# Value products four steps behind the scores in place of two, in the attention stage of a hybrid block on one Trainium2 core

## The reference

```python
def hybrid_layer(x, positions, ...):
    h = rmsnorm(x, g_norm_mix)
    proj = h @ w_in                       # split into 14 parts
    ...
    y_att = dsa_attention(aq, ak, av, iq, ik, iw)
    qk = jax.nn.silu(causal_depthwise_conv(jnp.concatenate([mq, mk], axis=-1), w_conv_mlstm, b_conv_mlstm))
    ...
    hm = mlstm_chunkwise(mq, mk, mv, i_pre, f_pre)
    y_mlstm = jax.nn.sigmoid(mo) * rmsnorm(hm, g_norm_mlstm_out)
    merged = jax.nn.sigmoid(ga) * (y_att @ w_proj_att) + jax.nn.sigmoid(gm) * (y_mlstm @ w_proj_mlstm)
    x = x + merged @ w_out
    return x + hierarchical_moe(rmsnorm(x, g_norm_moe), ...)
```

## Time and profile before

| | |
|---|---|
| three runs | 3398.79, 3401.74, 3405.67 us; median 3401.74 |
| the profiled execution | 3402.78 us, of which its span (first to last instruction) 3401.2 us |
| busy over the span | PE 87%, DVE 78%, ACT 58%, POOL 14% |
| mean granted clock of PE | 0.947 of full speed |
| `attend_and_recur`, flat steps | about 1212 to 1925 us of the span |

### The profile page before, as it was taken

One profiled execution on the slowest core, in us unless ns is written; L12 is line 12 of the kernel. 1 busy time (PEld: TensorE's weight loads), 2 busy tenths in 40 slices (PEclk: granted clock), 3 DMA queues, 4 the chain that ended last, 5 costly groups with the idle time before them and its releaser, 6 DMA issues. The chain is left out here.

```text
span 3401.2 us, 46483 instructions
## 1 busy us (share of the span) xinstructions
PE 2970.3 (87%) x13279; PEld 2273.1 (67%) x13280; DVE 2651.3 (78%) x4184; ACT 1982.4 (58%) x2803; POOL 490.5 (14%) x607
## 2 busy tenths in 40 slices
PE   7998899899899777888888689999399999999990
PEld 5766768588688544555555467877388888888870
DVE  6577589999899787888876555443699999999985
ACT  5322467676778365665656533332377777777770
POOL 0211110100000152222211100000111111111115
PEclk9999999999999978999999889999699999999995
DMA  3222533232222265435423375553478879677868
GB/s 124 87 75 75 141 118 121 91 115 91 59 69 77 74 143 134 115 94 109 90 65 56 110 207 172 165 172 104 178 267 309 331 279 377 217 253 257 308 250 342
DMA packets 378861, 546.05 MB, mean 161 GB/s; under 512 B 32528, under 2 KB 213440, under 8 KB 378576
## 3 DMA queue, kind: packets, MB, share of 16 engines
q1 hardware_dynamic: 346368, 434.02, 41.3%
q0 software_dynamic: 28448, 100.94, 8.0%
q10 hardware_dynamic: 3888, 9.18, 0.7%
HBM read 510.70 MB, written 138.19 MB: 191 GB/s over the span
## 5 line engine op out<-in xcount | busy, mean ns | idle before, releaser
L915 DVE TENSOR_TENSOR e_w_lo<-e_raw,e_w_hi 128x1024 fp32r<-128x1024 f32 x386 | 447.0, 1221 | 4.0 <-ACT e_w_hi L772 4.0
L1585 PE MATMUL x_ps<-h_hi,w_hi 128*128 128x512 f32 (+1 forms) x992 | 390.5, 394 | 5.6 <-PEq L90 4.5
L1585 PE MATMUL x_ps<-h_lo,w_hi 128*128 128x512 f32 (+1 forms) x992 | 388.8, 392 | 0.0
L1585 PE MATMUL x_ps<-h_hi,w_lo 128*128 128x512 f32 (+1 forms) x992 | 388.5, 392 | 0.0
L772 ACT CAST e_w_hi<-e_raw 128x1024 fp32r<-128x1024 f32 x386 | 376.7, 1052 | 5.5 <-PE e_pG L710 5.5
L1772 DVE TENSOR_SCALAR_CACHE_REDUCE x_relu<-x_score,x_cand 128x1024 uint8<-128x1024 f32 (+3 forms) x217 | 315.7, 1487 | 3.6
L1687 ACT ACTIVATE x_relu<-x_score,x_cand 128x896 int8<-128x896 f32 (+3 forms) x217 | 281.0, 1296 | 59.7 <-DVE x_cand L1779 59.5
L2379 ACT ACTIVATE t_probT<-t_ST 128x512 f32<-128x512 f32 x272 | 161.3, 593 | 175.6 <-PE t_ST L2195 173.1
L2410 DVE CUSTOM_DVE_ANT_0 t_junk<-t_L,t_mask 128x512 bf16<-128x512 f32 (+3 forms) x320 | 186.7, 607 | 85.4 <-PE t_L L2166 83.7
L710 PE MATMUL e_pG<-e_w_hi,e_x_hi 128*128 128x512 f32 x768 | 246.8, 403 | 3.6 <-DVE e_x_lo L910 3.6
L710 PE MATMUL e_pG<-e_w_lo,e_x_hi 128*128 128x512 f32 x768 | 242.5, 397 | 0.0
(11 more groups left out here) (424 smaller groups left out, 6814.0 us busy)
## 6 DMA issues: line engine op xcount, KB each, us to landing
e_raw<-in_w_exp_gate SPq DMA_DIRECT2D x392, 256.0 KB
e_raw<-in_w_exp_up SPq DMA_DIRECT2D x392, 256.0 KB
e_raw<-in_w_exp_down SPq DMA_DIRECT2D x192, 512.0 KB
projT<-x_out SPq DMA_DIRECT2D x120, 256.0 KB, 3.0
slot_out<-e_y POOLq DMA_DIRECT2D x48, 512.0 KB, 6.1
w_raw<-in_w_in SPq DMA_DIRECT2D x40, 512.0 KB
o_gate<-projT SPq DMA_DIRECT2D x32, 512.0 KB
slot_out<-x_zeros SPq DMA_DIRECT2D x31, 512.0 KB
```

What stands on the lines that cost most here:

```text
L915: nc.vector.tensor_tensor(w_lo[:, u, :], raw[:, u, :], w_hi[:, u, :].bitcast(F32), ALU.subtract).then_inc(gl, 1)
L1585: last = nc.tensor.matmul(ps[0:w, u % 4, :], wt[:, m % 2, kk, 0:w], ht[:, kk, q * 512:(q + 1) * 512], start=(kk == 0 and s == 0), stop=(kk ...
```

## The change

A constant `LAG = 4` sets how many flat steps the value products stand behind the scores; it was 2. To have room, `probT_hi` gets five buffers and `probT_lo` four (both had three); in exchange there are two output buffers in place of three, two buffers in place of three for the unused full output of the maximum (`junk`), and `SQ` of the recurrence shares its memory with `T2`. The copy out of `t_O` and, on SP, the store, the load of the queries four blocks ahead and the DMAs for the sums move with the value products, from one to three flat steps after the end of a pair.

```diff
+    LAG = 4
...
-        OU, DEC = sb("out", [AD + 1, 3, R4, P]), sb("m_DEC", [P, MH, NT])
+        OU, DEC = sb("out", [AD + 1, 2, R4, P]), sb("m_DEC", [P, MH, NT])
...
-        PH, PL = sb("probT_hi", [P, 3, 512], F32R), sb("probT_lo", [P, 3, 512], F32R)
+        PH, PL = sb("probT_hi", [P, LAG + 1, 512], F32R), sb("probT_lo", [P, LAG, 512], F32R)
...
-        junk = sb("junk", [P, 3, 512], BF16)
+        junk = sb("junk", [P, 2, 512], BF16)
...
+        SQ = T2
...
             for f in range(FLAT + 20):
-                s = ended(f, 1)
+                s = ended(f, LAG - 1)
                 if s is not None:
                     store(s)
                     n, v = STEPS[s]
                     if v == 1 and n + 4 < NT:
                         load(n + 4)
...
-                    if len(before) == 2:
+                    if len(before) == LAG:
                         values(*before.pop(0))
...
                     a.activation(den[:, :], N1[:, :, MD], ACT.Abs).then_inc(sq_ok, 1)
+                    if k:
+                        act.wait_ge(yt_ps, k)
                     a.activation(SQ[:, :, :], N1[:, :, 0:MD], ACT.Square).then_inc(sq_ok, 1)
...
             def probabilities_high(s, j):
-                if f >= 3:
-                    act.wait_ge(pv_ok, f - 2)
-                a.copy(PH[:, f % 3, :], PT[:, f % 3, :]).then_inc(ph_ok, 1)
+                if f >= LAG + 1:
+                    act.wait_ge(pv_ok, f - LAG)
+                a.copy(PH[:, f % (LAG + 1), :], PT[:, f % 3, :]).then_inc(ph_ok, 1)
...
             def out(s):
-                if s >= 3:
-                    act.wait_ge(y_st[s % 3], 48 * (s // 3))
+                if s >= 2:
+                    act.wait_ge(y_st[s % 2], 48 * (s // 2))
...
-                    if ended(f, 1) is not None:
-                        out(ended(f, 1))
+                    if ended(f, LAG - 1) is not None:
+                        out(ended(f, LAG - 1))
...
             def maximum(s, x, seen):
-                if seen >= 3:
-                    dve.wait_ge(mx_ok, seen - 2)
+                if seen >= 2:
+                    dve.wait_ge(mx_ok, seen - 1)
...
             def probabilities_low(f):
-                if f >= 3:
-                    dve.wait_ge(pv_ok, f - 2)
+                if f >= LAG:
+                    dve.wait_ge(pv_ok, f - LAG + 1)
```

More of the change, by code:

```diff
@@ L1899, in attend_and_recur @@
         CAUS = sb("m_caus", [P, P])
-        QW, AR, MP, KW, T1, T2, SQ = (sb("m_" + n, [P, MH, P]) for n in ("QW", "AR", "PT", "KW", "T1", "T2", "SQ"))
+        QW, AR, MP, KW, T1, T2 = (sb("m_" + n, [P, MH, P]) for n in ("QW", "AR", "PT", "KW", "T1", "T2"))
+        SQ = T2
         VO, CN, N1 = (sb("m_" + n, [P, MH, E1]) for n in ("VO", "CN", "N1"))
@@ L1912, in attend_and_recur @@
         mk_in = [sem(f"mask_in{b}") for b in range(4)]
-        y_st = [sem(f"y_stored{b}") for b in range(3)]
+        y_st = [sem(f"y_stored{b}") for b in range(2)]
         mk_set, l_ok, mx_ok, nm_ok, d_ok, st_ok, p_ok, ph_ok, pl_ok, pv_ok, ou_ok, vh_ok, vl_ok = (sem(n) for n in (
@@ L2041, in store @@
                     sp.dma_start(y_d[k * AD:(k + 1) * AD, 2 * v:2 * v + 2, n * P:(n + 1) * P],
[L2042 to L2044 removed]
+                                 OU[0:AD, s % 2, k::2, :]).then_inc(y_st[s % 2], 16)
+                sp.dma_start(sum_d[v * R4:(v + 1) * R4, n * P:(n + 1) * P].rearrange("(o h) n -> o h n", o=1), OU[AD:AD + 1, s % 2, :, :]
+                             ).then_inc(y_st[s % 2], 16)
             for f in range(FLAT + 20):
[L2046 removed]
+                s = ended(f, LAG - 1)
                 if s is not None:
@@ L2052, in _ @@
                     if v == 0 and n % 4 == 0 and n:
-                        for b in range(3):
-                            sp.wait_ge(y_st[b], 48 * len(range(b, s, 3)))
+                        for b in range(2):
+                            sp.wait_ge(y_st[b], 48 * len(range(b, s, 2)))
                         sp.dma_start(SUM[:, n // 4 - 1, :], sums(sum_d, n // 4 - 1)).then_inc(sum_in, 16)
@@ L2059, in _ @@
                 side(f)
-            for b in range(3):
-                sp.wait_ge(y_st[b], 48 * len(range(b, len(STEPS), 3)))
+            for b in range(2):
+                sp.wait_ge(y_st[b], 48 * len(range(b, len(STEPS), 2)))
             sp.wait_ge(rec_st, 16 * (NGRP - 1))
@@ L2205, in values @@
                     pe.wait_ge(ou_ok, s)
-                nc.tensor.matmul(O[0:AD + 1, :, :], VH[:, j, v, :], PH[:, f % 3, :], start=(j == 0), stop=False)
-                nc.tensor.matmul(O[0:AD, :, :], VL[:, j, v, :], PH[:, f % 3, :], start=False, stop=False)
+                nc.tensor.matmul(O[0:AD + 1, :, :], VH[:, j, v, :], PH[:, f % (LAG + 1), :], start=(j == 0), stop=False)
+                nc.tensor.matmul(O[0:AD, :, :], VL[:, j, v, :], PH[:, f % (LAG + 1), :], start=False, stop=False)
                 pe.wait_ge(pl_ok, f + 1)
-                nc.tensor.matmul(O[0:AD + 1, :, :], VH[:, j, v, :], PL[:, f % 3, :], start=False, stop=(j == n)).then_inc(pv_ok, 1)
+                nc.tensor.matmul(O[0:AD + 1, :, :], VH[:, j, v, :], PL[:, f % LAG, :], start=False, stop=(j == n)).then_inc(pv_ok, 1)
             def side(f):
@@ L2361, in probabilities_high @@
                 act.wait_ge(p_ok, at_st[s, j] + 1)
-                if f >= 3:
-                    act.wait_ge(pv_ok, f - 2)
-                a.copy(PH[:, f % 3, :], PT[:, f % 3, :]).then_inc(ph_ok, 1)
+                if f >= LAG + 1:
+                    act.wait_ge(pv_ok, f - LAG)
+                a.copy(PH[:, f % (LAG + 1), :], PT[:, f % 3, :]).then_inc(ph_ok, 1)
             def out(s):
                 act.wait_ge(pv_ok, FIRST[s + 1])
-                if s >= 3:
-                    act.wait_ge(y_st[s % 3], 48 * (s // 3))
-                a.copy(OU[:, s % 3, :, :], O[0:AD + 1, :, :]).then_inc(ou_ok, 1)
+                if s >= 2:
+                    act.wait_ge(y_st[s % 2], 48 * (s // 2))
+                a.copy(OU[:, s % 2, :, :], O[0:AD + 1, :, :]).then_inc(ou_ok, 1)
             shift_row(0)
@@ L2387, in _ @@
                     side(f)
-            out(len(STEPS) - 1)
             for f in range(FLAT, FLAT + 20):
+                if ended(f, LAG - 1) is not None:
+                    out(ended(f, LAG - 1))
                 side(f)
@@ L2407, in maximum @@
                 dve.wait_ge(l_ok, seen + 1)
-                if seen >= 3:
-                    dve.wait_ge(mx_ok, seen - 2)
-                v_.tensor_tensor_reduce(junk[:, seen % 3, 0:hi - lo], L[:, seen % 3, 0:hi - lo], MB[:, n % 4, lo:hi], 1.0, -3e38,
+                if seen >= 2:
+                    dve.wait_ge(mx_ok, seen - 1)
+                v_.tensor_tensor_reduce(junk[:, seen % 2, 0:hi - lo], L[:, seen % 3, 0:hi - lo], MB[:, n % 4, lo:hi], 1.0, -3e38,
                                         ALU.add, ALU.max, mxp[:, s % 2, h, p:p + 1]).then_inc(mx_ok, 1)
```

2 lines of the change are left out of this document (1 added, 1 removed).

## The result

The changed kernel takes 3416.18 us (median of 6 runs, 3411.97 to 3418.32), the kernel before, on the same chip, 3399.32. The ratio is 1.0044 (95% interval 1.0034 to 1.0054): slower by 15 us by the ratio (16.9 between the medians), where 9 us of gain were forecast. The profiled execution took 3416.5 us.

A forecast was written before the change was run, and what follows sets the result against it. The stage was taken as a chain of four engines waiting for one another, none saturated. Terms -21 + 5.5 + 1.5 + 4 + 1.1 = -9 us gave 3393 us, faster by 0.26%, range 3379 to 3412.

The forecast's parts named there:

- (1): Attention-and-recurrence stage: value products two steps later shorten DVE's waits for logits, a gain of 21 us (4 to 32).
- The term of 13 us at c+1: One step after a chunk's flat step c: scores come earlier, 1.1 us in each of 12 periods (0 to 17).
- The lower bound: Low end of the gain at c+1: 0 us, if the logit banks bind first.
- the start's own gain of 2 us: First 98 us of the stage: DVE idles 16 us, 10.6 of it on a DMA; 2 us gained.
- (2): After 1800 us: PE would wait longer for ScalarE's exponential by what it saved; gain 0 (up to 4 us).
- (3): SP's queue: later loads lose 5.5 us at load(4), 1.5 at load(5), 4 at the first chunk's loads.
- (4): Two output buffers: out(s) waits for the store two steps back, which is hidden; 3 us if not.
- (6): The junk ring, SQ on T2 and the low part's wait for values cost 0.
- (5): End of the stage: four value steps instead of two after the last scores, about 1.1 us later (0 to 2).
- C: Logit banks or ScalarE take the wait over at once: gains 10, losses 12, 3403 us; chance 0.20.
- B: Flat steps 6 and 12: late query and chunk loads stall 16.3 and 12.3 us, 3414 us; chance 0.12.
- D: Before m_Y at c+2: PE's longer wait halves its clock, 13 us over twelve periods, 3406 us; chance 0.08.

The follow-up runs named there:

- e3: Changed kernel with a lag of 4 only from flat step 30 to 205, else 2: 3397.6 us, 0.9983 of the kernel before.
- e1: Changed kernel with load(n + 4) issued one flat step after the end of a block, ahead of the store: 3400.57 us, 0.9992 of the kernel before.
- e4: Changed kernel with a lag of 4 only from flat step 206, else 2: 3409.36 us, 1.0022 of the kernel before.
- e7: Changed kernel with a lag of 2 throughout and the loads of chunks 13 to 15 held back: 3408.39 us, 1.0017 of the kernel before.
- e6: Changed kernel with the loads of chunks 12 to 15 ahead of the output store: 3409.48 us, 1.0027 of the kernel before.
- e12: e8 plus eight unread matmuls of constants on PE at c+14 of chunks 11 to 15: 3390.7 us, 0.9965 of the kernel before.
- e8: Changed kernel with the edits of e1 and e6 together: 3399.04 us, 0.9995 of the kernel before.
- e13: Changed kernel plus fourteen unread matmuls of constants on PE at c+14 of chunks 11 to 15: 3408.74 us, 1.0036 of the kernel before.
- e5: Changed kernel with a lag of 4 only below flat step 30, else 2: 3412.78 us, 1.0041 of the kernel before.
- e2: Changed kernel with a lag of 2 throughout, so all its other edits alone: 3399.06 us, 0.9997 of the kernel before.
- e9: e8 plus eight unread matmuls of constants on PE at c+12 of chunks 11 to 15: 3402.41 us, 1.0005 of the kernel before.

## Why the prediction was wrong

The sum had -21 + 5.5 + 1.5 + 4 + 1.1 = -9; measured is +15. Three steps failed: the gain of the middle was forecast 13 us too large, the start's loss 5 us too small, and the end, put at nothing, lost 7.5. Put right alone, only the first turns the sum of -9 into a loss, of 4 us; the second makes it -1.5, the third -4. Step by step:

**(1), value products later: the mechanism was right, the size was not.** Forecast 19 us for the middle; measured 5.8 (e3), and 4.5 between the means of the table. The term of 13 us at c+1 failed; it is the largest part of the miss. It took the exponential of c+13 as the next constraint and let it come 1.2 us earlier on average. But by the rows of waits PE met the logit banks first (42.6 us of new waits for a maximum), and ScalarE the `probT` ring, behind mask rows that it now reached earlier and waited for longer (25.2 us at c+12 over the middle, before 13.1). In chunk 2's period, against the earlier trace rows, its wait for the mask rows is 3.71 us. Behind it the copy out of the single `t_O` bank is late too, PE waits 1.84 us for that, and DVE still stands for logits:

```profile
1443.97 0.63 ACT L2334 ACTIVATE t_m_AR<-t_m_AR 128x512 f32<-128x512 f32 x1 [3.71 <-DVE t_m_AR L2489]
...
1446.88 0.66 PE L2208 MATMUL t_O<-t_probT_hi,t_v_hi 128*65 128x512 f32 x1 [1.84 <-ACT t_out L2374]
...
1448.75 0.56 DVE L2415 CUSTOM_DVE_ANT_0 t_junk<-t_L,t_mask 128x384 bf16<-128x384 f32 x1 [1.31 <-PE t_L L2168]
```

DVE's waits at c+1 fell from 17.2 to 13.3 us and those at c+7, where 6 us were forecast, from 19.9 to 10.9, but those at c+14 and c+0 rose from 3.9 to 11.8. The lower bound ("0, if the logit banks bind first") named the case that came. No run had a fourth logit bank or `probT` buffer, so that these rings are what holds is read from the waits and not tested. Nor is the start's own gain of 2 us: with early loads the start is 2.7 us under the 102.6 of a lag of two, but no run has early loads and a lag of two, and in e1 DVE's wait for the first chunk's loads is 7.3 us, 3.3 less than before the change.

**(2), "I take 0" after 1800: the mechanism was wrong.** Measured +7.5 us (e4). It was right that PE would wait longer by what it saved. It missed two things. The move of SP's queue was followed past the first chunk's loads, not past those of chunks 13 to 15, which stand right behind a moved store; imposed on a lag of two this costs 5.5 us (e7's end), taken back at a lag of four it returns 2.0 (e6). And a saved wait that gathers in one place costs the clock: with it held, 8.7 us come back (e12 against e8) and 5.3 (e13). The shares don't add: mended one at a time the two return 2.0 and 5.3 us, together 10.7 (143.8 to 133.1). With early loads alone the waits are still 2.0 to 3.5 us and the clock falls at all four; with the clock held alone the loads are still late. With both mended the end is 2 to 3 us shorter than with a lag of two (133.1 against 134.7 to 136.0), so a lag of four is not itself the loss there.

**(3), SP's queue: right place, right kind, somewhat too small.** Forecast 11 us of loads less 2; measured 13.9 (e5, 9 to 18), with 10.1 in the profile's start. That start was set against 106.0, the longest of the six with a lag of two; against the other five it is 12.3 to 13.5. `load(4)` cost 7.0 us for 5.5. For `load(5)` nobody waits, where 1.5 us were counted; DVE's wait for the first chunk's loads grew by 1.6 us, from 10.60 to 12.18, where 4 were. The unit load at 1277.32, which the prediction passed by without a price, cost DVE some 3 us more than before. This split is read from one profile; no run moved these loads one by one. That it is order, e1 shows: with the loads ahead of the stores no loss is left.

**(4) and (6)** held: e2 is at 0.9997. **(5)** was too large: from the last exponential to `m_Y` it is 3.2 us in place of 2.9, so 0.3 us where 1.1 were counted.

Of the rivals, C (little happens) was nearest for the gain. B had the sign and 3414 us, but by landings twice as long as those that came. D had the mechanism that decided the end, the half clock after a longer wait, put at c+2 of the middle. It acted at c+14 of chunks 11 to 14, where no logits fill PE; its sign, PEclk under 0.9 in the middle, did not come (0.91). The Trainium skill (page "TensorE: Matmul & The Clock Gate", section "HAM oscillation — how this bites in real kernels") describes that pattern for waits on a DMA, and advises a loop order that keeps PE at work ahead of them. The trace agrees that PE kept at work holds its clock: 1.00 in e12, where e6 has 0.50. The section's rule speaks of longer idle gaps than the 2.00 us after which the clock fell in e8; the measurement decides.

## What to carry to other kernels

When a consumer is moved to a later step, list all that its engine's queue issues behind it, in every period and not only the first: here stores that nobody awaits delayed loads that somebody does, for some 14 us at the start alone. Slack for one engine is worth what the next constraint leaves, so count rings (logit banks, `probT` buffers) before taking a wait's length as gain. And look where the saved waits gather: here idle pieces of PE of up to 1.6 us mostly kept its clock, most single ones of 1.9 us and more lost it, and where the half clock then lay on the path the stage paid for it in the microseconds behind.

## What the runs showed of the hardware

The four mask-row operations take DVE 1.13 us when GpSimd is idle (ten of the changed kernel's sixteen), 2.16 beside one 128x512 operation of GpSimd (before, at 1827.50), and 3.27 beside two (after, at 1831.75). Data that land late start both engines at the same moment (1867.17 and 1867.21), which makes a late load dearer than its delay. The Trainium skill (page "SBUF — State Buffer", section "SBUF: two separate sides") says that a DVE instruction with two inputs in SBUF and a GpSimd one that reads it exclude one another; the trace agrees. The pair of DMA issues of a store took SP 1.23 to 1.28 us in most places of the changed kernel, but 3.33 us at 1224.34 and 6.21 at 1318.81; why is not shown.

And the clock of PE fell to half at a single wait of 2.00 us in e8 and after one of 1.97 in e13, while it held after one of 1.74 us that followed 1.67 us of matmuls in e12. The length of one wait does not decide it alone: after the wait of 3.24 us in e9, and after one of 2.64 us in e2, it held:

```profile
1815.00:1822.00 7.00, 3.76 (x18) 2.16 (x19) 5.75 (x10) 1.87 (x5) 2.95 (x2) 1.00 0.13 39
```
